# Modulation's products over four column groups of the array, and another order of the scans' loads

## The reference

```python
mods = (jax.nn.silu(cvec) @ p['w_ada'] + p['b_ada'])[..., None, :]
sh1, sc1, g1, sh2, sc2, g2 = jnp.split(mods, 6, axis=-1)
h = _rmsnorm(x, p['norm1_g']) * (1 + sc1) + sh1
o, new_states = _mixers(h, p, states, grid)      # RG-LRU, RWKV-7 and GLA side by side
x = x + g1 * o
h = _rmsnorm(x, p['norm2_g']) * (1 + sc2) + sh2
x = x + g2 * _expert_choice_ffn(h, p)            # 16 experts, expert choice
```

## Time and profile before

| what | value |
|---|---|
| median of three runs | 3469.64 us (3467.23 to 3474.12) |
| the profiled execution's own time | 3468.2 us |
| its span, first to last instruction | 3466.3 us |
| mean granted TensorE clock | 0.953 |
| busy: PE, PEld, DVE, ACT, POOL | 3119.8, 2853.6, 2273.6, 1609.6, 878.8 us |
| DMA over the span | 561.43 MB, mean 162 GB/s |
| modulation stage | 0 to 46 us |
| scans | 949 to 1735 us |
| a half block of `w_ada` | 1024.0 KB |

### The profile page before, as it was taken

How to read it: one execution, slowest core, us unless ns; L and a number is a source line. 1 busy time by engine, 2 the same in 40 slices (tenths; PEclk the granted TensorE clock), 3 DMA queues, 4 the chain that set the end, 5 groups by cost and what they waited for, 6 DMA issues and landing times. The chain is left out here.

```text
span 3466.3 us, 90868 instructions
## 1 busy us (share of the span) xinstructions
PE 3119.8 (90%) x37105; PEld 2853.6 (82%) x37105; DVE 2273.6 (66%) x4485; ACT 1609.6 (46%) x2917; POOL 878.8 (25%) x1232
## 2 busy tenths in 40 slices
PE   7899989999689999999958971899999999999996
PEld 3887867767579889999947750899999999999996
DVE  4575548996468788888867758555555555555555
ACT  2312756665545444555456530344444444444454
POOL 0110100000056666666622200111211111111213
PEclk8999989999889999999979975899999999999998
DMA  5465335665554554444376622555665655555685
GB/s 178 123 187 175 87 94 190 208 200 160 165 130 113 131 145 106 103 108 109 68 192 187 181 88 85 196 184 184 198 204 189 190 188 190 183 184 187 204 297 186
DMA packets 583428, 561.43 MB, mean 162 GB/s; under 512 B 211550, under 2 KB 527262, under 8 KB 582138
## 3 DMA queue, kind: packets, MB, share of 16 engines
q1 hardware_dynamic: 547084, 447.27, 43.2%
q0 software_dynamic: 36016, 109.52, 10.7%
HBM read 418.33 MB, written 138.33 MB: 161 GB/s over the span
## 5 line engine op out<-in xcount | busy, mean ns | idle before, releaser
L3440 DVE TENSOR_TENSOR exp_wlo<-exp_raw,exp_whi 128x2048 fp32r<-128x2048 f32 x192 | 440.0, 2293 | 362.9 <-ACT exp_whi L3341 355.3
L3341 ACT CAST exp_whi<-exp_raw 128x2048 fp32r<-128x2048 f32 x189 | 359.9, 1904 | 75.7 <-DMA exp_raw<-in_w_up 74.0
L1030 PE MATMUL mix_acc<-proj_hThi,mix_wlo 128*128 128x448 f32 (+3 forms) x920 | 356.3, 387 | 14.5 <-DVE mix_wlo L1398 14.5
L1030 PE MATMUL mix_acc<-proj_hTlo,mix_whi 128*128 128x448 f32 (+3 forms) x920 | 334.7, 364 | 0.0
L1030 PE MATMUL mix_acc<-proj_hThi,mix_whi 128*128 128x448 f32 (+3 forms) x920 | 334.3, 363 | 0.0
L3270 PE MATMUL moe_o<-moe_hidhi,exp_wlo 128*128 128x272 f32 x1024 | 306.8, 300 | 2.6 <-DVE moe_hidlo L3554 2.6
L3270 PE MATMUL moe_g<-moe_xThi,exp_wlo 128*128 128x272 f32 x1024 | 298.9, 292 | 1.0 <-DVE moe_xTlo L3444 1.0
L3270 PE MATMUL moe_o<-moe_hidhi,exp_whi 128*128 128x272 f32 x1024 | 297.1, 290 | 0.0
L3270 PE MATMUL moe_u<-moe_xThi,exp_wlo 128*128 128x272 f32 x1024 | 296.7, 290 | 0.0
L3270 PE MATMUL moe_u<-moe_xThi,exp_whi 128*128 128x272 f32 x1024 | 296.4, 289 | 0.0
L3270 PE MATMUL moe_g<-moe_xThi,exp_whi 128*128 128x272 f32 x1024 | 296.3, 289 | 0.0
(11 more groups left out here) (392 smaller groups left out, 8552.3 us busy)
## 6 DMA issues: line engine op xcount, KB each, us to landing
exp_raw<-in_w_gate SPq DMA_DIRECT2D x64, 1024.0 KB, 5.1
exp_raw<-in_w_up SPq DMA_DIRECT2D x64, 1024.0 KB, 5.1
exp_raw<-in_w_down SPq DMA_DIRECT2D x64, 1024.0 KB, 5.1
scn_plain<-rec SPq DMA_DIRECT2D x68, 384.0 KB, 3.7
rec<-mix_arena SPq DMA_DIRECT2D x24, 896.0 KB, 4.4
proj<-mix_out POOLq DMA_DIRECT2D x88, 224.0 KB, 2.5
scn_grc<-grec SPq DMA_DIRECT2D x136, 128.0 KB, 3.9
mix_arena<-in_w_ada SPq DMA_DIRECT2D x12, 1024.0 KB, 6.8
```

Of the source, the lines that this page charges most:

```text
L1030: mm = pe.matmul(acc[n % ACCS][0:width, 0:tn], wt[:, k, 0:width], hT[hp][:, k, t0:t0 + tn], start=k == 0 and i == 0, stop=k == KD - 1 and ...
L3341: act.copy(w[k % RING][0][:, :, :], raw[k % RAW][:, :, :]).then_inc(hi_done[k % RING], 1)
L3440: dve.tensor_tensor(w[k % RING][1][:, :, :], raw[k % RAW][:, :, :], w[k % RING][0][:, :, :], ALU.subtract).then_inc(lo_done[k % RING], 1)
```

## The change

In the modulation stage the four products of a half block no longer go to the same two partitions of PSUM but to partitions 0, 32, 64 and 96 and the ones behind (`GAP * i`), so that each lies in another group of 32 columns of the array; each group sums two of a block's eight products. The accumulators and `out` now have 98 rows and are set to zero by VectorE at the start; the bias goes to rows 0 and 1 and is loaded after the zeroing, behind the second load of `w_ada`. The selector `ones` becomes 98 x 128 with four ones a column, made by summing four columns of the identity, so the spreading product also adds the four parts. VectorE's bias addition works on 98 partitions instead of 2.

In the scans the three tables are issued by ScalarE. `load(c)` issues first the two `plain` of both directions, then the four `grc`, then the values. `plain` gets its own semaphore `plain_in`, for which `strict` waits; the wait for `rec_in` (now `SV` and `Vc` alone) moves to `state_seen`. `grec_in` still counts `grc` and `gv` together.

```diff
--- before.py
+++ after.py
@@ -117,16 +117,20 @@
 def stage_modulation(nc, parts, c, c_ctx, w_ada, b_ada):
 
     NB, RING = MOD_FIRST // BANK, 4
+    GROUPS, GAP = KD // 2, P // 4
+    ROWS = GAP * (GROUPS - 1) + 2
+    assert GROUPS == 4
     assert MOD_FIRST == 2 * D and NB == 4
     with Stage(nc, "mod") as st:
         cvec, sil = st.sb("cvec", [P, 2, KD]), st.sb("sil", [P, KD, 2])
         w = [st.sb(f"w{r}", [P, KD // 2, BANK]) for r in range(RING)]
-        out = st.sb("out", [2, MOD_FIRST])
-        ones = st.sb("ones", [2, 2, P])
+        out = st.sb("out", [ROWS, MOD_FIRST])
+        ones, picks = st.sb("ones", [ROWS, 2, P]), st.sb("picks", [ROWS, 2])
         acc, spread = [st.ps(f"acc{u}") for u in range(2)], [st.ps(f"spread{u}") for u in range(4)]
         cvec_in, bias_in, silu_done, ones_done = (st.sem(n) for n in ("cvec_in", "bias_in", "silu_done", "ones_done"))
         w_in = [st.sem(f"w_in{r}") for r in range(RING)]
         half_done, biased, spread_mm = st.sem("half_done"), st.sem("biased"), st.sem("spread_mm")
+        acc_zeroed, out_zeroed, picked = st.sem("acc_zeroed"), st.sem("out_zeroed"), st.sem("picked")
 
         def cols(b):
             return slice(b * BANK, (b + 1) * BANK)
@@ -145,9 +149,11 @@
                         sp.wait_ge(half_done, n - RING + 1)
                     sp.dma_start(w[n % RING][:, :, :], wv[:, n % 2 * (KD // 2):(n % 2 + 1) * (KD // 2), cols(n // 2)]).then_inc(w_in[n % RING], 16)
                     if n == 0:
+                        sp.dma_start(parts.ident[:, :], parts.sources[3]).then_inc(parts.ident_in, 16)
+                    if n == 1:
+                        sp.wait_ge(out_zeroed, 1)
                         for v in range(2):
                             sp.dma_start(out[v:v + 1, :], b_ada[:, 0:MOD_FIRST]).then_inc(bias_in, 16)
-                        sp.dma_start(parts.ident[:, :], parts.sources[3]).then_inc(parts.ident_in, 16)
                 sp.dma_start(parts.g_row[:, :], parts.sources[2].to_broadcast([P, D])).then_inc(parts.g_in, 16)
                 parts.load_x(sp, 0)
                 parts.load_x(sp, 1)
@@ -173,6 +179,7 @@
                             pe.wait_ge(parts.scale_done, v + 1)
                         pe.matmul(spread[2 * (b // 2) + v][:, :], ones[:, v, :], out[:, cols(b)], start=True, stop=True).then_inc(spread_mm, 1)
                 pe.wait_ge(silu_done, 1)
+                pe.wait_ge(acc_zeroed, 2)
                 for b in range(NB):
                     if b >= 2:
                         pe.wait_ge(biased, b - 1)
@@ -180,7 +187,7 @@
                         pe.wait_ge(w_in[n % RING], 16 * (n // RING + 1))
                         for i in range(KD // 2):
                             k = n % 2 * (KD // 2) + i
-                            mm = pe.matmul(acc[b % 2][0:2, :], sil[:, k, :], w[n % RING][:, i, :], start=k == 0, stop=k == KD - 1)
+                            mm = pe.matmul(acc[b % 2][GAP * i:GAP * i + 2, :], sil[:, k, :], w[n % RING][:, i, :], start=k < GROUPS, stop=k >= GROUPS)
                             if i == KD // 2 - 1:
                                 mm.then_inc(half_done, 1)
                     if b:
@@ -189,9 +196,14 @@
 
             @block.vector
             def _(dve):
+                for u in range(2):
+                    dve.memset(acc[u][0:ROWS, :], 0.0).then_inc(acc_zeroed, 1)
+                dve.memset(out[:, :], 0.0).then_inc(out_zeroed, 1)
                 dve.wait_ge(parts.ident_in, 16)
                 for v in range(2):
-                    dve.tensor_copy(ones[:, v, :], parts.ident[0:2, v:v + 1].to_broadcast([2, P])).then_inc(ones_done, 1)
+                    dve.tensor_reduce(picks[:, v:v + 1], parts.ident[0:ROWS, v:ROWS:GAP], AX.X, ALU.add).then_inc(picked, 1)
+                    dve.wait_ge(picked, v + 1)
+                    dve.tensor_copy(ones[:, v, :], picks[:, v:v + 1].to_broadcast([ROWS, P])).then_inc(ones_done, 1)
 
                 def scaled(b):
                     dve.wait_ge(parts.g_in, 16)
@@ -202,7 +214,7 @@
                 dve.wait_ge(bias_in, 32)
                 for b in range(NB):
                     dve.wait_ge(half_done, 2 * (b + 1))
-                    dve.tensor_tensor(out[:, cols(b)], acc[b % 2][0:2, :], out[:, cols(b)], ALU.add).then_inc(biased, 1)
+                    dve.tensor_tensor(out[:, cols(b)], acc[b % 2][0:ROWS, :], out[:, cols(b)], ALU.add).then_inc(biased, 1)
                     if b == 3:
                         scaled(2)
                 scaled(3)
@@ -1789,7 +1801,7 @@
         def rings(name):
             return [st.sem(f"{name}_{u}") for u in range(NB)]
         eye_there = st.sem("eye_there")
-        con_in, rec_in, grec_in = st.sem("con_in"), rings("rec_in"), rings("grec_in")
+        con_in, rec_in, grec_in, plain_in = st.sem("con_in"), rings("rec_in"), rings("grec_in"), rings("plain_in")
         lm_done, u0_done, t0_done, kr_done, rk_done, bk_done = (each(n) for n in (
             "lm_done", "u0_done", "t0_done", "kr_done", "rk_done", "bk_done"))
         l_mm, kr_mm, rk_mm, bk_mm, x_mm, kT_mm = (st.sem(n) for n in ("l_mm", "kr_mm", "rk_mm", "bk_mm", "x_mm", "kT_mm"))
@@ -1806,7 +1818,7 @@
             "att_a", "att_b", "masked", "folded", "att_sum", "go_mm", "go_done", "gs_done"))
         go_out = [st.sem2(f"go_out{g}") for g in range(G)]
         gstate_out, gstate_in = st.sem("gstate_out"), st.sem("gstate_in")
-        N_REC, N_GREC = 16 * 4 * G, 16 * (GN + 2) * G
+        N_PLAIN, N_REC, N_GREC = 16 * G, 16 * 3 * G, 16 * (GN + 2) * G
 
         def v3(ap):
             return ap.rearrange("p (j t) -> p j t", j=UN)
@@ -1829,18 +1841,18 @@
         with st.block() as block:
             @block.sync
             def _(sp):
-                sp.dma_start(con[:, :], consts_d).then_inc(con_in, 16)
-                sp.dma_start(gcon[:, :], gla_consts_d[:, 0:WG]).then_inc(con_in, 16)
-                sp.dma_start(total[:, :, :, :], decay).then_inc(con_in, 16)
-
                 def load(c):
                     u, at = c % NB, reached(c)
                     for g in range(G):
-                        js, rows = slice(UN * g, UN * (g + 1)), slice(at[g] * C, at[g] * C + C)
+                        js = slice(UN * g, UN * (g + 1))
                         chunk_rec = rec[g, :, at[g]:at[g] + 1, :, :]
-                        sp.dma_start(plain[u][:, js, :].rearrange("p j w -> p (j w)"), chunk_rec.rearrange("p c j w -> p (c j w)")).then_inc(rec_in[u], 16)
+                        sp.dma_start(plain[u][:, js, :].rearrange("p j w -> p (j w)"), chunk_rec.rearrange("p c j w -> p (c j w)")).then_inc(plain_in[u], 16)
+                    for g in range(G):
+                        rows = slice(at[g] * C, at[g] * C + C)
                         for j in range(GN):
                             sp.dma_start(grc[u][:, g, j, :].rearrange("p (f t) -> p f t", t=C), grec[j, :, :, rows]).then_inc(grec_in[u], 16)
+                    for g in range(G):
+                        rows = slice(at[g] * C, at[g] * C + C)
                         sp.dma_start(SV[u][HIGH, g, :, :, :].rearrange("t j h v -> t (j h v)"), v_rows[rows, :]).then_inc(rec_in[u], 16)
                         for h in range(2):
                             sp.dma_start(Vc[u][HALVES[h], g, :, :], v_rows[rows, :].rearrange("t (j h v) -> h t j v", h=2, j=UN)[h]).then_inc(rec_in[u], 16)
@@ -1954,6 +1966,9 @@
 
             @block.scalar
             def _(act):
+                act.dma_start(con[:, :], consts_d).then_inc(con_in, 16)
+                act.dma_start(gcon[:, :], gla_consts_d[:, 0:WG]).then_inc(con_in, 16)
+                act.dma_start(total[:, :, :, :], decay).then_inc(con_in, 16)
                 act.wait_ge(con_in, 48)
 
                 def magnitudes(g, c):
@@ -2052,7 +2067,7 @@
                 def strict(c):
 
                     u = c % NB
-                    pe.wait_ge(rec_in[u], N_REC * (c // NB + 1))
+                    pe.wait_ge(plain_in[u], N_PLAIN * (c // NB + 1))
                     if c > 1:
                         pe.wait_ge(go_done[1], c - 1)
                     for g in range(G):
@@ -2120,6 +2135,7 @@
                 def state_seen(c):
 
                     u, S = c % NB, Ss[segment(c)]
+                    pe.wait_ge(rec_in[u], N_REC * (c // NB + 1))
                     for g in range(G):
                         pe.wait_ge(kr_done[g], c + 1)
                     if c == NCH_CTX:
```

## The result

The changed kernel took 3445.91 us (median of four runs, 3440.40 to 3449.68) against 3470.44 for the kernel before on the same chip: a ratio of 0.992, 95% interval 0.990 to 0.9941. That is 24.5 us by the medians. The profiled execution is one of those runs, 3448.97 us, and its span went from 3466.3 to 3447.2, 19.1 us less. Its sum was 14.8 us.

The account below looks back on a forecast made before the run. No single engine bounds the whole; TensorE bounds modulation, transfers next. Modulation 10.0 plus scans' start 4.8 makes 14.8 us off 3468.2, 3453.4, plus 1.4 to the runs' median: 3454.8 us, range 3448 to 3463.

Parts of the forecast that it names:

- the gate in between: Scans, chunk 0: TensorE's keys_turned waits for GpSimd's differences, then ScalarE's magnitudes and copies, holding the gain to 4.8 us.
- without overlap: Rival, modulation: column groups do not overlap, that stage gains 0, 4.8 us remain, 3464.8 us; chance 0.12.
- with passes that run out one by one: Rival, modulation: each pass ends before the next group's begins, 15.6 us more, 3480.4 us; chance 0.04.
- with nothing left at the gate (as a total): Rival, scans' start: gv no earlier and clock low, only the modulation's 10.0 us gained, 3459.6 us; chance 0.09.
- Part 1: Modulation stage, products in column groups: the stage ends at 35.7 instead of 45.69, 10.0 us gained.
- starts are in order, so I take pairs ... 5 slots: Modulation: passes overlap two at a time, so a half block takes 5 slots, 2.17 us against 3.47.
- full overlap: Rival, modulation: all four groups at once, 2 slots a half block, 11.6 us gained there, 3453.2 us; chance 0.08.
- another rival: Rival, modulation: TensorE's clock stays low to the stage's end, 5.2 us gained there, 3459.6 us; chance 0.07.
- Part 2: Scans, tables on ScalarE and new load order: chunk 0 gains 4.8 us, the remaining 32 chunks nothing.
- the stated bound of 2: Scans, chunk 0: lower bound of 2 us gained if TensorE's clock also falls in the 2 us wait.
- 0.8 earlier: Scans, chunk 0: the last gv lands at 962.6, so GpSimd's differences start 0.8 us earlier.
- the remaining 32 chunks: ... their order is worth nothing: Scans after the start: loads run three chunks ahead, so their order was taken to gain 0 us.

Follow-up runs that it names:

- e8: The changed kernel with two column groups instead of four for the modulation products; 3462.4 us, ratio 0.9915 to the kernel before.
- e11: The changed kernel unchanged, run again as reference on another chip; 3459.60 us, ratio 0.9916 to the kernel before.
- e3: The changed kernel unchanged, run again as reference on its chip; 3444.12 us, ratio 0.9918 to the kernel before.
- e5: The changed kernel, but loads from the third chunk on issue both plain, then the values, then grc; 3465.07 us, ratio 0.9931 to the kernel before.
- e6: The changed kernel, but loads from the third chunk on issue grc, then the values, then both plain; 3475.33 us, ratio 0.9949 to the kernel before.
- e9: The changed kernel, but gv counts on rec_in, so GpSimd's differences wait for grc alone; 3450.48 us, ratio 0.9897 to the kernel before.
- e12: The same kernel as e9, run once more; 3453.31 us, ratio 0.9912 to the kernel before.
- e4: The changed kernel, but loads from the third chunk on issue in the old order, direction by direction; 3458.57 us, ratio 0.9950 to the kernel before.
- e7: The changed kernel, but the three tables are issued by SyncE ahead of the loads, as before; 3461.32 us, ratio 0.991 to the kernel before.
- e10: The changed kernel without loads from the third chunk on, reusing the first three chunks' data; 3426.07 us, ratio 0.9821 to the kernel before.

## Why the prediction was right and wrong

**Right.** That the passes overlap in column groups; that SyncE's memset wait, the memsets and the reductions are hidden; that the stage's end follows TensorE and DMA closely; TensorE's first scan products 5 us earlier (+13.7 to +8.9) and yet only a part of that at chunk 0; the gate in between, GpSimd's differences and then ScalarE's copies; the added wait in state_seen costs nothing that shows (no run takes it out by itself). The rivals without overlap, with passes that run out one by one, and with nothing left at the gate (as a total) are out.

**Part 1, the step "starts are in order, so I take pairs ... 5 slots".** It failed. All four groups run at once, two slots (after) and four with two groups (e8). The rival "full overlap" had 11.6 us, and 12.1 were measured. Its sum used 3.04 us per half block and ended at 34.0; with 2.67 it would end at 7.37 + 7 x 2.67 + 0.9 + 4.75 = 31.7, by the same working. The measured end is 33.58: the low clock up to some 25 us, which was part of another rival, costs the 1.9 us between. Its signature is in the timeline: block 3 starts at 26.99 without an idle note, so it waits for block 2 and its spread, not for data. e11 bears this out: with the clock up by 15.2 us the same code waits for the last half block's data, and its last scaling ends at 31.19. So the mechanism was full overlap with the transfers as the bound, and how much of it a run shows hangs on when the clock rises.

The Trainium skill, "TensorE: Matmul & The Clock Gate", Part 3, says under "The mechanism" that a weight load overlaps running matmuls only where the row group differs, which would have given no overlap here. The rows contradict it for this form: four passes with the same row group start within 0.02 us. The same section has matmuls start strictly in order, on which my pairs stood too; e8's four slots contradict that. The 2.38x for three column tiles in "Measured speedup vs the span model" of that Part was nearer than my pairs: four tiles gave 8 slots to 2, 4x, where TensorE is at work.

**Part 2, chunk 0: 4.8 predicted, 1.3 measured, outside the stated bound of 2.** The failed term is GpSimd's "0.8 earlier". It was 1.3 later, because the issue of gv was costed at the old pace less 1.33 us; with all plain and grc transfers ahead of it SyncE's issues themselves take longer, 4.43 us for four grc. A further 1.4 went to TensorE's clock in the attention, the bound that was named; where the same code ran it at the fast pace (e3, e5, e6, e8) chunk 0 gained 2.6 to 3.6 us. e9 and e12 show the wait for gv from the other side: with gv taken out of it, GpSimd starts at +10.7 to +11.1 and chunk 0 ends at +42.9 to +43.6.

**Part 2, "the remaining 32 chunks: ... their order is worth nothing".** This is the step that put the time outside the range. It argued from waits on semaphores only, and there are indeed none. But the profile of before had the sign of another cost: TensorE's 24 us of "issue" waits in the steady chunks, and a queue of instruction packets beside the data. What the step left out is that data transfers, in time themselves, make TensorE's instructions come late. The order of the loads was worth 8.6 us between the two profiled executions and 14.5 us between the medians of e3 and e4. Taking 12.1 + 1.3 + 8.6 gives 22.0 of the 24.5 us of the medians; the rest is within the spread of the runs. Without this term the time would have looked right, and by luck: 12.1 + 1.3 = 13.4 against the predicted 14.8, from one part too small and another too large.

**What is shown and what is inferred.** Shown by edits: that the order of the later loads sets the scans' time (e4 against e3, e6 against e7; e5 alone would not say so, its 745.3 us being near e8's 744.6, which has the new order); that the gaps almost vanish without loads (e10). Shown by counting: that TensorE's gaps stand where its instructions run out, and end behind the landing of the next packet. Inferred: that data on the same engines holds back the start of these packets. The traces have when a packet ran, not when it was asked for, and no run changed the instruction loads themselves. Open is which property of the loads does it, their place, their sum at one time or their form. The size also scatters: the same order had stretches of 728.9 to 730.9 us on two chips and 734.0 to 744.6 on three others, and the time at packet ends goes with it (34.0 to 35.1 and 39.0 to 47.5).

## What to carry to other kernels

A product with only a few output rows can be spread over PSUM's 32-partition groups, if the sum of the groups can be folded into something that follows anyway; expect the full factor only where TensorE is the bound. What comes next is data (two groups served here as well as four) and TensorE's clock, whose rise came anywhere between 13.4 and 25 us in runs of the same code and was worth some 2 us. Transfers that are always in time are not free: where TensorE runs through long unrolled code, look for its "issue" waits, count whether they stand a whole instruction packet apart, and try other places for the bulk transfers. Here both large loads side by side at the front of a step did better than one in the middle of it. And a semaphore that counts several transfers starts its waiter at the slowest; count apart what is needed apart.

## What was not expected of the hardware

- 32 float32 products of 512 columns in four column groups: eight passes in two slots (0.85 us a slot at the low clock); with two groups four slots, where starts in program order would have given seven.
- TensorE's instructions arrive in packets of 16 KB, one in 4.3 us here and one for 256 of its records, and 351 of its 376 gaps over 0.5 us stand exactly at such a packet's end. 29 of 30 end 1.2 to 1.8 us after one has landed. At a DMA share of 0.14 there were 7 such gaps, at 0.43 to 0.45 between 18 and 38.
- With short bursts of products TensorE stayed at its 1.2 GHz level to 13.4 us in one execution and to 25 in another of the same code, while in the kernel before it rose right after 11.4 us, having worked without a gap since 7.17.
- Four issues of grc, 128 KB each, took SyncE 4.43 us at the stage's start and 2.56 a chunk later.
